# A two-block sequence model on one NeuronCore: the first feed-forward norm folded into its matmuls, a head group's inversion rebuilt, and the first head group's start re-ordered

## What is computed

```python
def first_block(...):
    ...                                   # pooling and attention, gates, merged
    mix = jnp.einsum('bsd,de->bse', merged, w_out)
    x = x + rmsnorm(mix, g_post_mix)
    h2 = rmsnorm(x, g_pre_mlp)
    a = jnp.square(jax.nn.relu(jnp.einsum('bsd,df->bsf', h2, w_up)))
    ff = jnp.einsum('bsf,fd->bsd', a, w_down)
    x = x + rmsnorm(ff, g_post_mlp)

def gdn_mixer(h, ...):
    proj = h @ w_in                       # q, k, v, z, and 16 + 16 small columns b, a
    qkv = silu(causal_depthwise_conv(qkv, conv_w))
    beta = sigmoid(b)
    g = -exp(a_log) * softplus(a + dt_bias)
    o = gated_delta_rule_chunked(l2norm(q) * 128 ** -0.5, l2norm(k), v, beta, g)
    return (rmsnorm_2(o, out_norm) * silu(z)) @ w_out

def gated_delta_rule_chunked(q, k, v, beta, g):    # per head, per chunk
    m = (k * beta) @ k.T * strict_decay
    u, w = solve(m + I, [v * beta, k * beta * exp(gc)])   # unit lower triangular
    attn = q @ k.T * decay
    ...                                   # then the state is carried from chunk to chunk
```

## Time and profile before

| | us |
|---|---|
| median of 3 runs | 2053.23 |
| lowest and highest | 2047.31, 2053.25 |
| the profiled execution, device time | 2043.85 |
| its span | 2042.0 |
| mean granted clock of PE | 0.963 |
| PE, DVE, ACT, POOL busy | 1886.5, 998.3, 819.8, 725.6 |

### The profile page before, as it was taken

The page is one execution under the profiler, slowest core; times in us unless marked ns, Lnnn a source line. Parts: engine busy times, 40 slices in busy tenths (PEclk is TensorE's granted clock), DMA queues, the critical chain, the costliest instruction groups (busy, mean ns, idle before and its releaser), DMA issues.

```text
span 2042.0 us, 30297 instructions
## 1 busy us (share of the span) xinstructions
PE 1886.5 (92%) x11493; PEld 1564.0 (77%) x11629; DVE 998.3 (49%) x1678; ACT 819.8 (40%) x1478; POOL 725.6 (36%) x454
## 2 busy tenths in 40 slices
PE   6999999799999996988989999999978999999995
PEld 4677777578787875987989988998967777777773
DVE  6522213441321325665765765676555555555564
ACT  4555542341323233633633643452434333334332
POOL 3223244343534342370381273255134212222223
PEclk9899999899999998989989998998989999999997
DMA  5111123122323231220220231131132101211111
GB/s 176 52 52 57 60 90 103 42 84 91 110 80 108 82 104 46 87 74 1 86 74 22 66 84 43 45 95 52 42 105 73 52 32 54 71 51 51 62 51 41
DMA packets 73228, 140.35 MB, mean 69 GB/s; under 512 B 30592, under 2 KB 40320, under 8 KB 72992
## 3 DMA queue, kind: packets, MB, share of 16 engines
q1 hardware_dynamic: 72256, 133.98, 20.6%
q10 hardware_dynamic: 864, 4.87, 0.6%
HBM read 129.20 MB, written 9.63 MB: 68 GB/s over the span
## 4 chain that ended last, share of the span: by engine, by line
PE 42%; DVE 6%; POOL 5%; issue 4%; ACT 3%; DMA 0%; ACTq 0%; POOLq 0%; SPq 0%; DVEq 0%
PE ps L313 9%; PE ps L314 8%; PE ps L315 8%; PE ps L2551 3%; POOL wsp L308 2%; PE ps L2507 2%; PE ps L2514 2%; POOL ov L678 1%; PE ps L2541 1%; DVE aux_f L1431 1%; POOL work L674 1%; PE ps L2219 1%; PE ps L2326 1%; PE ps L2364 1%; PE ps L2240 1%
## 5 line engine op out<-in xcount | busy, mean ns | idle before, releaser
L308 POOL TENSOR_TENSOR wsp<-raw,wsp 128x1024 fp32r<-128x1024 f32 x231 | 557.0, 2415 | 1208.7 <-ACT wsp L303 1208.7
L313 PE MATMUL ps<-h_split,wsp 128*128 128x264 f32 (+1 forms) x1488 | 525.2, 353 | 25.8 <-POOL wsp L308 11.4
L314 PE MATMUL ps<-h_split,wsp 128*128 128x264 f32 (+1 forms) x1488 | 512.4, 344 | 0.0
L315 PE MATMUL ps<-h_split,wsp 128*128 128x264 f32 (+1 forms) x1488 | 511.5, 344 | 0.0
L313 PEld LDWEIGHTS ps<-h_split,wsp 128*128 128x128 f32 x1488 | 289.5, 195 | 67.7 <-issue 34.4
L314 PEld LDWEIGHTS ps<-h_split,wsp 128*128 128x128 f32 x1488 | 290.0, 195 | 31.5
L315 PEld LDWEIGHTS ps<-h_split,wsp 128*128 128x128 f32 x1488 | 288.8, 194 | 32.5
L303 ACT ACTIVATE wsp<-raw 128x1024 fp32r<-128x1024 f32 x231 | 240.9, 1050 | 105.1 <-PE ps L315 103.8
L313 PE MATMUL ps<-y_split,wsp 128*128 128x512 f32 (+1 forms) x496 | 194.8, 393 | 12.9 <-DVE y_split L475 5.8
L314 PE MATMUL ps<-y_split,wsp 128*128 128x512 f32 (+1 forms) x496 | 191.2, 385 | 0.0
L315 PE MATMUL ps<-y_split,wsp 128*128 128x512 f32 (+1 forms) x496 | 191.0, 385 | 0.0
(11 more groups left out here) (359 smaller groups left out, 3012.5 us busy)
## 6 DMA issues: line engine op xcount, KB each, us to landing
raw<-in_w SPq DMA_DIRECT2D x231, 512.0 KB, 3.5
m_home<-ov SPq DMA_DIRECT2D x16, 256.0 KB, 3.5
x_home<-x_res ACTq DMA_DIRECT2D x1, 2112.0 KB, 6.5
x_res<-x_home ACTq DMA_DIRECT2D x4, 528.0 KB, 7.1
x_res<-in_x SPq DMA_DIRECT2D x4, 512.0 KB, 5.4
out<-x_res SPq DMA_DIRECT2D x8, 256.0 KB, 2.0
mats<-in_mats SPq DMA_DIRECT2D x1, 640.0 KB, 7.4
rope<-in_rope ACTq DMA_DIRECT2D x1, 528.0 KB
```

What stands on the lines that cost most here:

```text
L308: pool.tensor_tensor(wsp[:, s, 1, :], raw[:, s, :], wsp[:, s, 0, :].bitcast(F32), ALU.subtract).then_inc(lo_ready, 1)
L313: pe.matmul(o, wh, xh, start=start, stop=False)
L314: pe.matmul(o, wh, xl, start=False, stop=False)
L315: return pe.matmul(o, wl, xh, start=False, stop=stop)
```

## The change

It has four parts.

1. Norm n2: DVE and ACT apply the gain alone, in the pass that updates X; PE averages the squares between the slices of up tiles 0 and 1 (tile 1 lags by three slices); 1/rms is multiplied in when DVE reads an up tile. ACT then squares and copies. Round 0 is written out, the loop has two rounds.
2. Group 0: the small projection and panel 0 share each slice, the gate steps lie between pieces of panel 1, and the decay rows come behind panel 2. ACT's, DVE's and SP's programs follow.
3. The inversion: level 5 works in blocks of 32 rows (`in_quarters`), levels 5 and 6 read M without a mask, the masks that are left (7 of 15) have three buffers. `spread_16` goes from GpSimd to DVE, `attend_mask` and T's level 0 for the meta tokens from DVE to GpSimd, the other `attend` calls in front of the inversion.
4. Fillers: the q k^T grams stand in front of panel 9, gate tile 2 goes in 16 slices into steps 9 to 14 and behind them, gate tile 3 into chunk 0, and the output tiles start in chunk 1.

The diff, cut to its core:

```diff
 def in_halves(l, c):
-    return bool(c) and l < LEVELS - 1
+    return bool(c) and l == LANE_LEVEL
+def in_quarters(l, c):
+    return bool(c) and l == LANE_LEVEL + 1
+MASKED = [s for s, (l, c) in enumerate(STEPS) if l == LANE_LEVEL or not c]
+LAG = 3
+GATE_FROM = 9
...
 # GpSimd, per group
+                def mask(k):
+                    l, c = STEPS[MASKED[k]]
...
+                    if k >= 3:
+                        pool.wait_ge(sem("g_q"), gst(g, NS, MASKED[k - 3] + 1))
...
+                for k in range(3):
+                    mask(k)
...
+                for k in range(3, NM):
+                    mask(k)
+                pool.wait_ge(sem("g_t16"), gst(g, LATER, LATER))
+                low(8)
+                for c in range(CHUNKS):
+                    attend_mask(c)
+                for j in range(9, 12 if first else 16):
                     low(j)
...
 # ScalarE, passage and rounds
-            norm_squares(act, "n2", lambda k: X[:, k, REAL], N1, ready=lambda k: added("nA", k))
+            for k in range(KT):
+                gained_high(act, "n2", k, HS[:, 0, k, REAL], X[:, k, REAL], "g_pre_mlp", ready=added("nA", k))
+                norm_square(act, "n2", lambda m: X[:, m, REAL], N1, k)
...
-                    act.activation(relu[b], PS[:, m % 4, :], ACT.Relu).then_inc(sem("ff_relu"), 1)
                     act.wait_ge(sem("ff_relu"), c)
-                    act.activation(Y[:, 0, m, REAL], relu[b], ACT.Square).then_inc(sem("ff_hi"), 1)
+                    act.activation(relu2[b], relu[b], ACT.Square).then_inc(sem("ff_sq"), 1)
+                    act.wait_ge(sem("ff_sq"), c)
+                    act.activation(Y[:, 0, m, REAL], relu2[b], ACT.Copy).then_inc(sem("ff_hi"), 1)
...
 # VectorE, rounds
-                    dve.wait_ge(sem("ff_relu"), c)
-                    dve.tensor_tensor(relu2[b], relu[b], relu[b], ALU.mult).then_inc(sem("ff_sq"), 1)
+                    dve.wait_ge(used, turn(P_FF + m + 1, r, 16))
+                    dve.scalar_tensor_tensor(out=relu[b], in0=PS[:, m % 4, :], scalar=0.0, in1=N1["rs"],
+                                             op0=ALU.max, op1=ALU.mult).then_inc(sem("ff_relu"), 1)
...
 # ScalarE, group 0
+                if first:
+                    gates_front()
+                    split_ahead(1)
+                    gates_middle()
+                    conv_exp(0)
+                    decay_high()
+                    decay_sums()
+                    lnexp(0)
+                    decay_rest()
+                    park()
+                    l2_square(0)
+                    conv_exp(1)
+                    lnexp(1)
+                    split_ahead(2)
+                    l2_square(1)
+                    decays(1)
+                    decays(2)
...
 # TensorE, group 0
+                if first:
...
+                        last = mm3t(pe, 6, *w, HS, kt, kt == 0, kt == KT - 1)
...
+                        last = mm3t(pe, 0, *part(0, kt), HS, kt, kt == 0, kt == KT - 1)
+                    last.then_inc(used, 1)
+                    project(1, 2, 0, 3)
+                    gates_turned()
+                    project(1, 2, 3, 6)
+                    decay_sums()
+                    project(1, 2, 6)
+                    pe.wait_ge(sem("g_conv"), 1)
+                    project(2, 0)
+                    pe.wait_ge(sem("rows_moved"), 16 + 64)
...
+                    pe.wait_ge(sem("g_conv"), 2)
+                    project(3, 2, 0, 4)
+                    pe.wait_ge(sem("g_eabs"), 2 * HG)
+                    l2_sum(0)
...
 # TensorE, all groups
-                project(9, 6)
+                for c2 in range(1, CHUNKS):
+                    grams(6, c2, 2).then_inc(sem("g_kq"), 1)
+                pe.wait_ge(sem("g_conv"), gst(g, 8, 8))
+                project(9, 2)
...
+                    if in_quarters(l, c):
+                        for h in range(HG):
+                            for x, y in QUARTERS:
+                                last = pe.matmul(PS[x, s % 2, h * P + y.start:h * P + y.stop],
+                                                 left[y, h, x], U[c][y, h, y], start=True, stop=True)
...
+                    if s > GATE_FROM:
+                        gate_slices(2 * (s - GATE_FROM) - 1)
                     if s:
                         join(s - 1)
+                    if s >= GATE_FROM:
+                        gate_slices(2 * (s - GATE_FROM))
...
-                            out_tile((0, 3, 5)[c - 2])
-                            norm_o(c - 1)
+                        out_tile(*((0,), (2,), (4, 0, 2), (5,))[c - 1])
+                        norm_o(c - 1)
```

More of the change, by code:

```diff
@@ L722, in gdn_group, with attend_mask @@
-                for j in range(10, 12 if first else 16):
+                    if k >= 3:
+                        pool.wait_ge(sem("g_q"), gst(g, NS, MASKED[k - 3] + 1))
+                    pool.tensor_tensor(CL[k % 3][0:n, :, 0:n], M[c][0:n, :, 0:n], level_mask(l, n),
+                                       ALU.mult).then_inc(sem("g_cl"), 1)
+                def attend_mask(c):
+                    n = tokens(c)[1]
+                    a = AT[c][0:n, :, 0:n]
+                    pool.wait_ge(sem("g_at"), gst(g, CHUNKS, c + 1))
+                    pool.tensor_tensor(a, a, mats[0:n, TRI_U:TRI_U + 1, 0:n].to_broadcast([n, HG, n]), ALU.mult)\
+                        .then_inc(sem("g_at2"), 1)
@@ L890, in ff_round @@
                         square_ff(m - 1)
-            with act.Fori(0, 3) as r:
+            ff_round(0, first=True)
+            with act.Fori(1, 3) as r:
                 ff_round(r)
@@ L930, in gdn_group, with decay_rest, park @@
+            def decay_rest():
+                act.wait_ge(sem("ba_dve"), 8)
+                act.activation(sm[:, 4, :, :], sm[:, 4, :, :], ACT.Exp).then_inc(sem("ba_act"), 1)
+            def park():
+                for k in range(KT):
+                    act.wait_ge(*added("nB", k))
+                act.dma_start(x_home, X).then_inc(sem("x_moved"), 16)
             def gdn_group(g, first):
@@ L1345, in _, with low_ff @@
             norm_sum_step(dve, "nA", N1, 7)
-            norm_add(dve, "nA", lambda k: mixf[:, k, :], "g_post_mix", N1, REAL)
+            def low_ff(k):
+                gained_low(dve, "n2", k, HS[:, 1, k, REAL], X[:, k, REAL], "g_pre_mlp", HS[:, 0, k, REAL])
             dve.memset(tiny[:, 8:9], 0.0).then_inc(sem("ff_add"), 8)
-            norm_apply(dve, "n2", lambda k: X[:, k, REAL], "g_pre_mlp", N1, hs(REAL))
+            dve.wait_ge(sem("norm_rs"), nth("nA", 1, 1))
+            for k in range(KT):
+                if k >= 2:
+                    dve.wait_ge(*added("nA", k - 2))
+                dve.scalar_tensor_tensor(out=N1["tmp"][k % 2], in0=mixf[:, k, :], scalar=col("g_post_mix", k),
+                                         in1=N1["rs"], op0=ALU.mult, op1=ALU.mult)\
+                   .then_inc(sem("norm_branch"), 1)
+                if k % 2 == 0:
+                    dve.wait_ge(sem("norm_branch"), nth("nA", k + 1, among=ADDS))
+                    dve.tensor_tensor(X[:, k, REAL], X[:, k, REAL], N1["tmp"][0], ALU.add)\
+                       .then_inc(sem("norm_added"), 1)
+                else:
+                    if k > 1:
+                        low_ff(k - 2)
+                    low_ff(k - 1)
+            low_ff(KT - 1)
+            dve.wait_ge(sem("norm_rs"), nth("n2", 1, 1))
             dve.wait_ge(sem("acc_zero"), 1)
@@ L2022, in ff_round @@
                     last.then_inc(used, 1)
-            with pe.Fori(0, 3) as r:
+            ff_round(0, first=True)
+            with pe.Fori(1, 3) as r:
                 ff_round(r)
@@ L2240, in gdn_group @@
                                 last = pe.matmul(PS[r, s % 2, h * P + r.start:h * P + r.stop],
-                                                 CL[s % 2][r, h, r], U[c][r, h, r], start=True, stop=True)
+                                                 left[r, h, r], U[c][r, h, r], start=True, stop=True)
                     else:
```

527 lines of the change are left out of this document (292 added, 235 removed).

## The result

The changed kernel takes 2038.61 us (median of 15 runs, 2022.94 to 2046.97), the kernel before 2055.07 (15 runs, 2042.79 to 2060.83). The ratio is 0.9913, interval 0.9893 to 0.9934, so some 18 us are won. The forecast was 47, and the time lies above the range of 1988 to 2028. The profiled execution took 2041.9, its span is 2040.1 (before: 2042.0) and its mean granted clock 0.950, where it was 0.963. PE is busy longer than before, though it has no more to do.

A forecast was written before the change was run, and what follows sets the result against it. TensorE (PE), busy 92% of the span, was taken as the bound. Terms of -7.5, +0.6, -7 and -33.4 summed to -47.3 us, taking 2053.2 to 2006, with a range of 1988 to 2028.

The forecast's parts named there:

- Part 1: Passage from first mixer into the feed-forward: earlier up matmuls win 7.5 us; waits for DVE's up-tile eviction cost 0.6.
- Part 2: Start of group 0: reordered work and one slow start gain 9 us, ACT's queue loses 2; -7.
- Panel 9: Wait before panel 9 in four groups: grams fill it, -8 us; granted clock no longer falls behind it, -6.
- Masks: Inversion: PE no longer waits for GpSimd's mask into F in three groups, -1.4 us together.
- The spreads: Four DVE spreads ahead of the inversion end before join 0 needs them; no cost, +1 us a group if late.
- Level 5: Inversion's level 5 in 32-row pieces: a call costs 0.47 to 0.94 us; taken as -0.5 a group, -2.
- The tail: Last level of each inversion and just behind: gate slices hold the clock and waits go, -21 us.
- part 3: The four groups: panel 9, clock behind it, masks, level 5, inversion's end and recurrence, -33.4 us together.
- rival 2: Inversion: level 5's smaller pieces let the clock fall from step 5; +8.6 us a group, 2067 in all, chance 0.06.
- The recurrence: Recurrence behind the inversion: one filler fewer, so chunks wait; +2 us in group 0, +1 in each other, +5.

The follow-up runs named there:

- e1: Changed kernel with the gate tile's slices, two a step, from step 5 of the inversion instead of step 9; 2008.1 us, ratio to the kernel before 0.9765.
- e9: Changed kernel with ScalarE's issue of the rope transfer ahead of the four transfers of X instead of behind them; one run, 2023.9 us.
- e4: Kernel before with nothing changed but level 5 of the inversion in 32-row pieces; 2065.2 us, ratio to the kernel before 1.0046.

## Why the prediction was wrong

**Part 1, -6.9: right.** From nA's mean to nB's 386.55 became 379.82, -6.7, and between 379.4 and 380.8 in all kernels built on the change. The first up matmul stands at 393.4 and not at 391.7, but the mixer had ended 1.9 later, and a mean stands between the slices at once:

```profile
386.71 1.12 PE L429 MATMUL ps<-work,mats 128*128 128x512 f32 x2 [2.18 <-DVE work L406]
393.43 0.77 PE L327 MATMUL ps<-h_split,wsp 128*128 128x512 f32 x1 [5.59 <-DVE h_split L490]
```

That is 6.7 after the mean, forecast 6.9. The third panel begins at 414.3, 27.6 after the mean (26.8 forecast, 34.6 before). In the forecast's sum the terms give 411.4 and not 411.6, and four times 0.17 is 0.7 and not 0.6; the two slips cancel but for 0.1. The relu eviction on VectorE cost less than the 0.6: PE's four waits make 3.5 in all (`DVE work L1447` in the rows below) and were 3.3. The kernel before had these waits, the second one for panel 9:

```profile
PE ps L313 <- ACT work L884: 3.3, 4, 0.9
PE ps L313 <- POOL wsp L308: 11.4, 4, 2.8
```

**Part 2, -7: right in the mechanism, 3 too much.** The end of panel 2 comes 28.2 after the first small matmul. Then the decay rows cost 1.71 of wait and about 1.0 of work, which makes 30.9 (39.7 before, 31 forecast). ScalarE's queue cost more than the 2 that I took:

```profile
817.12 0.50 PE L2221 MATMUL ps<-decay_r,ones_r 2*128 2x512 f32 x4 [1.71 <-DMA decay_r<-g_home]
...
842.66 1.76 PE L2207 MATMUL ps<-ov,mats 128*128 128x264 f32 x4 [2.17 <-ACT ov L1001]
```

and a window behind the second:

```profile
844.00:846.00 2.00, 2.00 (x10) 1.90 (x10) 1.53 (x3) 1.35 (x2) 0.57 (x1) 0.50 0.38 37
```

The wait of 2.17 is as sized; that the clock falls behind it, for 3.4 us, was missing (1.7). To the inversion 8.6 are won, of which panel 9 of this group has 4.3 (its wait of 2.85 and 3.4 of slow clock, less 1.95 for the grams that now stand there). It leaves -4.3 for part 2.

**Panel 9, -8 and -6: right, the second 2.4 too small.** PE's waits over the span in the changed kernel (us in total, times, longest):

```profile
PE ps L327 <- DVE work L1447: 3.5, 4, 1.0
PE ps L327 <- POOL wsp L322: 3.3, 3, 1.1
PE ps L2445 <- POOL aux_f L717: 3.2, 4, 0.8
```

The wait for GpSimd's low half was 11.4 in four groups and is 3.3: -8.1. The clock does not fall behind it in any group, so all of the 8.4 is won. In group 2:

```profile
1187.00:1189.00 2.00, 2.00 (x17) 2.00 (x18) 2.00 (x4) 0.73 (x1) 2.00 (x2) 1.00 0.78 78
```

**Masks, -1.4: right. The spreads, 0: +3.2.** The last of the rows above names GpSimd, but its masks for this call were ready long before. The VectorE instruction that PE's call of step 2 needs, the third of `turned_16`, and that call, in group 1:

```profile
1032.73 1.75 DVE L1598 TENSOR_TENSOR aux_f<-work,mats 128x512 f32<-128x512 f32 x1
1034.66 0.68 PE L2445 MATMUL ps<-aux_f,ov 64*64 64x64 f32 x16 [0.84 <-POOL aux_f L717]
```

Its mask, the third (`ov`), was done at 1029.44. VectorE's instruction ends at 1034.48, and PE starts 0.18 later, the same 0.18 in all four groups. It is late because two of the `spread_16` that the change gave to VectorE stand ahead of it (1.35), and because it took 1.75, where the fourth took 0.69. The prediction had this as "if late, +1 a group" and put it at nothing. It is 0.8 a group, and PE no longer waits for a mask.

**Level 5, -2: the call was sized at its good end and better.** From start to start a call takes 0.48 (1204.17 to 1204.65, the price at which pieces overlap was 0.47), 0.72 before: 7.7 in four groups.

**The tail, -21: this step failed.** Group 1 behaves as forecast: its inversion and its rest stay at full clock, the tail gives some 3.9 of the 4.9 (worked out as what is left of the group's change after the other terms), and the group takes 8.7 less than before, where the terms of part 3 gave some 8.1. The argument behind it was that small calls alone let the clock fall and that larger ones between them hold it. The runs bear that out, and just that I didn't apply to steps 5 to 8, where the change puts calls of a quarter of the area and no slice. The tail term took the clock to be at 1.00 when the slices begin, and they begin at step 9 (1209.47), 4.6 us after the fall in step 7. They don't lift a clock that has fallen as long as small calls stand between them. Three falls at 12.1 are 36 us; without them the execution would have taken 2005.6, and e1, which has no long fall, took 2006.7 in its profiled execution. That was rival 2, with 0.06, and its condition came about in three groups of four. Its price was a little high: a group with a fall came out at +3.1 against before (group 2), not +8.6. The pieces do overlap (-1.9 where the price has +2.1), and the clock behind panel 9, which that price leaves out, gives 1.7 a group.

What should have raised its chance was in the rows: the clock falls in the earlier trace rows while PE runs 64x64 calls, at 1.95 busy of 2. I took one sentence against the rival (each step has its transposes of 128x128) for enough. They are there in the changed kernel too (1205.13) and don't hold the clock.

The fall at 1205 has PE busy 1.89 and 1.93 of 2 us in its windows, as in the earlier trace rows. The Trainium skill, "TensorE: Matmul & The Clock Gate", section "HAM oscillation — how this bites in real kernels", names idle gaps of PE as what brings the clock down; this trace disagrees with gaps as the only cause.

**The recurrence, +5: right in sign, a third of the size.** The rest of group 1 went from 139.8 to 131.4, by 8.4. Slices moved out (48 matmuls of 0.121, 5.8), panel 9 (1.7 of wait and 1.7 of clock, less 1.95) and the slow clock behind the inversion (2.8 us of it, 1.4 lost) make 8.7, so the recurrence gave back 0.3 in this group, where 1 was forecast.

**Not in the sum: the latent attention, +6.7.** It was taken as unchanged. 3.5 are the rope issue, 1.7 the longer slow start behind it, and 1.5 come later, in the first latent group. With e9's order the latent attention is back at 515.4; the wait (3.4) is the order's, the rest is in part a matter of where else the clock fell.

**The account**, by the stretches of the first table: -47.3 forecast; +36.3 for three falls; +6.7 for the latent attention; +2.8 for the start of group 0 with its panel 9 (8.6 won, 11.4 forecast); -2.7 for the four groups from there on, which without the falls win 31.7 where 29.0 were forecast; +0.2 for part 1; and +2.0 for a mixer and a norm n3 that ended later in this execution (the mixer's end lies between 383.7 and 391.2 in these profiles). That is -2.0, and the two profiled executions differ by -1.9.

## What to carry over

Cutting a small matmul to its useful rows saves time on paper, 0.24 us a call here, and cost 12 us each time that the smaller calls let PE's clock fall. Put full-size work between them from the first one on, not behind them, and look at the granted clock of a stretch before sizing anything in it. Compare the stages that a change doesn't touch as well: here they took back 6.7 us, about half of it by one DMA issue on ScalarE. And read a wait against the program: the cause that a row or a total suggested was another for PE's wait in step 2 and for most of e4's time.

## What the hardware showed that I had not expected

- The clock fell with PE busy 1.93 of 2 us, during 32-row calls, with transposes of 128x128 between them. It stayed at 0.50 for 30 us through a mix of full-size matmuls and small calls, though the same mix ran at 1.00 in group 1. All the long falls ended only when the small calls of the inversion were over.
- Whether it falls differs between executions of the same instructions (three groups in one, two in e9, whose groups are the same). The changed kernel's 15 runs go from 2022.9 to 2047.0 at mean clocks of 0.962 and 0.948; how many falls each had was seen only in the profiled one.
- An issue of the same transfer took ScalarE 0.37, 0.69 or 3.5 to 4.5 us, by its place in the program.
